# Choosing the branch hint in the middle of a product: a TensorE program that jumps between eleven copies of an expert's code

## What is computed

```
gate = jnp.minimum(xb @ w_gate[e] + b_gate[e], SWIGLU_LIMIT)
up = jnp.clip(xb @ w_up[e] + b_up[e], -SWIGLU_LIMIT, SWIGLU_LIMIT)
act = gate * jax.nn.sigmoid(SWIGLU_ALPHA * gate) * (up + 1.0)
y = act @ w_down[e] + b_down[e]
```

## Time and profile before

| what | value |
|---|---|
| median of 3 runs | 2039.57 us (2031.48, 2039.57, 2040.16) |
| the profiled execution, its own time | 2035.33 us |
| its span from first to last instruction | 2033.6 us |
| granted clock of TensorE, mean | 0.987 |
| PE busy | 1957.0 us, 96% of the span |
| the expert stage | from about 506 to 2017 us |

### The profile page before, as it was taken

How to read it: one execution, slowest core, us unless ns; L and a number is a source line. 1 busy time by engine, 2 the same in 40 slices (tenths; PEclk the granted TensorE clock), 3 DMA queues, 4 the chain that set the end, 5 groups by cost and what they waited for, 6 DMA issues and landing times.

```text
span 2033.6 us, 40238 instructions
## 1 busy us (share of the span) xinstructions
PE 1957.0 (96%) x17569; PEld 1578.1 (78%) x17570; DVE 571.7 (28%) x1108; ACT 283.8 (14%) x457; POOL 283.1 (14%) x481
## 2 busy tenths in 40 slices
PE   8999988998899999999999999999999999999996
PEld 4444456555897798889778999987987878889996
DVE  3115667354222121222212222222221222121214
ACT  2001245111001001101100111111010110100103
POOL 0001233176101000000000010010000000101003
PEclk9999999998999999999999999999999999999998
DMA  4210021312978889998999988899999998887855
GB/s 176 84 42 1 1 94 44 127 69 95 330 264 301 307 277 339 336 326 290 356 348 336 314 300 283 294 359 350 313 351 322 335 347 292 282 280 250 288 170 202
DMA packets 232704, 501.98 MB, mean 247 GB/s; under 512 B 8822, under 2 KB 9487, under 8 KB 232498
## 3 DMA queue, kind: packets, MB, share of 16 engines
q1 hardware_dynamic: 219024, 454.53, 62.3%
q0 software_dynamic: 13424, 44.36, 8.9%
q10 hardware_dynamic: 50, 0.01, 0.0%
HBM read 463.70 MB, written 35.23 MB: 245 GB/s over the span
## 4 chain that ended last, share of the span: by engine, by line
PE 92%; issue 3%; DVE 2%; DMA 2%; ACT 1%; SPq 0%; POOL 0%; POOLq 0%; DVEq 0%
PE ps L1742 33%; PE ps L1751 23%; PE ps L1778 12%; PE ps L1515 8%; PE ps L1653 5%; PE ps L1509 3%; PE ps L1765 2%; PE ps L1553 1%; PE ps L1771 1%; DVE soft L1056 1%; ACT hT L782 1%; DMA qk<-x_rows 1%; PE ps L1673 1%; PE ps L1592 0%; DMA w_ring<-in_w_in 0%
## 5 line engine op out<-in xcount | busy, mean ns | idle before, releaser
L1751 PEld LDWEIGHTS ps<-hT,qk 128*64 128x64 f32 x4608 | 234.0, 138 | 26.9 <-issue 26.4
L1751 PE MATMUL ps<-hT,qk 128*64 128x128 f32 (+3 forms) x4608 | 239.1, 266 | 15.6 <-issue 13.8
L1778 PE MATMUL ps<-w_ring,hT 128*128 128x512 f32 x576 | 251.8, 593 | 0.0
L1742 PE MATMUL ps<-hT,qk 128*128 128x136 f32 (+5 forms) x1792 | 236.1, 295 | 9.4 <-issue 9.4
L1742 PEld LDWEIGHTS ps<-hT,qk 128*128 128x128 f32 x1792 | 234.4, 193 | 13.0 <-issue 13.0
L1742 PE MATMUL ps<-hT,w_ring 128*128 128x136 f32 (+5 forms) x1792 | 235.4, 292 | 2.9 <-DVE x L1303 1.5
L1742 PEld LDWEIGHTS ps<-hT,w_ring 128*128 128x128 f32 x1792 | 230.9, 190 | 5.2 <-issue 4.6
L1778 PEld LDWEIGHTS ps<-w_ring,hT 128*128 128x128 f32 x576 | 107.5, 190 | 126.7 <-issue 126.3
L609 POOL DMA_INDIRECT x_rows<-x,hT x44 | 70.3, 1598 | 788.2 <-ACT x L887 385.6
L1515 PE MATMUL ps<-hT,w_ring 128*128 128x512 f32 x384 | 168.9, 595 | 1.3 <-DMA w_ring<-in_w_in 1.3
L1281 DVE TENSOR_TENSOR hT<-ps,early 128x512 f32<-128x512 f32 (+1 forms) x64 | 51.7, 808 | 414.6 <-PE ps L1742 208.3
(11 more groups left out here) (261 smaller groups left out, 1667.3 us busy)
## 6 DMA issues: line engine op xcount, KB each, us to landing
w_ring<-in_w_down SPq DMA_DIRECT2D x64, 2048.0 KB, 8.9
qk<-in_w_gate SPq DMA_DIRECT2D x32, 2048.0 KB, 8.3
qk<-in_w_up SPq DMA_DIRECT2D x32, 2048.0 KB, 10.5
v<-in_w_gate SPq DMA_DIRECT2D x32, 2048.0 KB, 10.6
u_all<-in_w_up SPq DMA_DIRECT2D x32, 2048.0 KB, 9.6
x<-in_b_down SPq DMA_DIRECT2D x32, 512.0 KB
w_ring<-in_w_in SPq DMA_DIRECT2D x3, 2048.0 KB, 8.9
x<-in_x SPq DMA_DIRECT2D x8, 512.0 KB, 9.5
```

Of the source, the lines that this page charges most:

```text
L1742: ins = pe.matmul(bank[:, m, 0:n], w[g][:, k, m * P:(m + 1) * P], rhs[:, k, 0:n], start=k == 0, stop=k == KC - 1)
L1751: ins = pe.matmul(bank[part, m, 0:n], w[g][:, k, m * P + part.start:m * P + part.stop], rhs[:, k, 0:n], start=k == 0, stop=k == KC - 1)
L1778: ins = pe.matmul(ps[:, 2 * (g % PAIRS), :], aT[:, k, 0:P], w[g][:, k, :], start=k == 0, stop=k == KC - 1)
```

## The change

The decision tree moves. It now stands between the two parts of product 4, ahead of the wait at line 1873, runs over all twelve targets (the eleven widths and the end) in every case, and isn't split by `ONE_BLOCK` any more. Behind product 4 stays only the second turn, where the next expert is wide.

```
                         product(4, aT, early)
                     else:
                         rows_of(4, range(KC // 2))
+
+                    hints = {}
+                    call(hints, after, 0, len(WIDTHS))
                     pe.wait_ge(a_ready, e * 2 + 2)
                     pe.sem_inc(passed, 1)
                     (product(4, aT, late) if two_blocks else rows_of(4, range(KC // 2, KC))).then_inc(group_done, 1)
 
-                    hints = {}
                     with pe.If(after > ONE_BLOCK):
-                        with pe.If(after > len(WIDTHS) - 1):
-                            call(hints, after, len(WIDTHS), len(WIDTHS))
-                        with pe.Else():
+                        with pe.If(after < len(WIDTHS)):
                             pe.wait_ge(xT_ready, 2 * e + 3)
                             pe.sem_inc(passed, 1)
                             turn_in(1).then_inc(turn_mm[1], 1)
-                            call(hints, after, ONE_BLOCK + 1, len(WIDTHS) - 1)
-                            pe.sem_inc(passed, 1)
                         pe.sem_inc(passed, 1)
                     with pe.Else():
                         pe.sem_inc(turn_mm[1], 1)
-                        call(hints, after, 0, ONE_BLOCK)
                     ready(5)
```

## The result

The changed kernel takes 2016.19 us (median of 5 runs, 2014.49 to 2018.40) against 2036.12 (5 runs, 2031.48 to 2040.16) of the kernel before on the same chips: a ratio of 0.990, interval 0.9889 to 0.9911. Its profiled execution has a span of 2012.8 us, 20.8 under the span before.

The account below looks back on a forecast made before the run. PE is busy 1957.0 of 2033.6 us; code-fetch gaps at body heads and their half-clock stretches cost 24 us. Terms -2.3 - 2.6 - 1.7 - 4.1 + 7.0 + 1.0 + 1.5 + 0.9 = -0.3; forecast 2036, range 2022 to 2046.

Parts of the forecast that it names:

- Step 1: Between the second turn and product 5: the tree leaves, PE's gaps at seven wide-to-wide exits go, -2.3 us.
- Step 2: The tree's new place in product 4: PE's queued work covers its 1.4 us, cost 0.
- Step 3: Wide tails, boundary earlier through six added instructions a body: 168->96 -2.6, 144->120 -1.7, 168->144 -4.1 us.
- Step 4: 108 body's branch chain past a boundary, hint and branch apart: +7.0 us at one 108->128, +1.0 at 108->96.
- Step 5: Entries of the 128 and 160 bodies: shorter first blocks give less cover, +1.5 and +0.9 us.
- Step 6: Two 96->128 exits: branch's block entered 1.3 us earlier, worth 5.3 us each or nothing; taken as 0.
- rival A: At body exits, the hint acts when issued, wherever its branch stands; nearly all head gaps go: 2011 to 2015, chance 0.12.
- B: As forecast, but the two 96->128 exits gain from an earlier fetch: -11 us, 2024 to 2026, chance 0.12.
- if the 96->128 gaps vanish: Sign in the profile after, at the heads of the 128 body: gaps gone there would mean the hint-acts-earlier rivals hold.
- Step 7: Last exit, 180->end: early fetch lost, but the end waits on output DMAs; cost 0, at worst 2.6 us.
- C: Slower: double misses at narrow exits and 160 entries, wide-tail gains absent: +25 us, 2060, chance 0.08.
- D: Only two blocks are held, so hinted blocks are pushed out at up to 13 wide exits: +49 us, 2084, chance 0.02.

Follow-up runs that it names:

- l6_late: Kernel before with six more counter increments in product 4 of every body, so bodies start as in the changed kernel, hint where it was: ratio 0.9906.
- part 3: Changed kernel with the 128 body moved back by 2, 4 and 6 instructions by the code's length: 2014.07, 2012.78 and 2013.12 us.
- m128_s20: Changed kernel with never-run code placed to move only the 128 body 20 instructions back in its block, by the code's length: 2028.67 us.
- m128_s8: Changed kernel with never-run code placed to move only the 128 body 8 instructions back in its block, by the code's length: 2029.93 us.
- al128: Changed kernel with never-run code making every body whole blocks long, each starting in the middle of a block: 2044.11 us.
- al8_head: `al8` with 100 of its unused instructions moved ahead of the first tree, so the first body's hint and branch share a block: 2004.26 us.
- l0_early: Changed kernel with six increments fewer in each body's tree, so bodies start as in the kernel before, hint early: ratio 0.9967.
- al8: Changed kernel with never-run code making every body whole blocks long, each starting on a block boundary by the stalls' count: 2008.42 us.

## Why the prediction was wrong

**Held.** Step 1: the tree's seven gaps ahead of product 5 are gone. The runs give the whole move of the tree as 1.1 (within the noise), 4.1 and 6.1 us in three layouts, where I had 2.3. Step 2, cost 0: nothing in the timeline speaks against it. Step 3 held: the gaps at 168->96 (two), 144->120 (of which it had left 0.5) and 168->144 went, and the half-clock stretch behind the last of them too. They went in `l6_late` as well, where only the layout was changed.

**Step 4 failed**, the +7.0 and +1.0 at the 108 exits. No gap came at the first 108->128; its last branch took 0.47 us:

```profile
L1806 PEldq COMPARE_BRANCH  x4: 67/72/465, 793.1 to 793.5; - x4
```

I had fixed all positions by one stall in the 128 body, and carried it over to bodies ahead of it. But by the rule of part 3, in the kernel before the 120 body would begin 5 ahead of a boundary and is moved, so that the 96 and 108 bodies stand 5 instructions lower than my count had them. With that the taken branch of the changed 108 body stands 2 instructions ahead of the boundary and not behind it, in the block of its hint.

**Step 5 failed**, +1.5 and +0.9. I had the 128 body 4 instructions and the 160 body 8 ahead of a boundary; each would begin within 16 of one (10 and 4 by the corrected count) and is moved onto it. In place of the shortest first block the 128 body got the longest. This one error is worth most of the 20 us: 12.5 and 13.7 by `m128_s20` and `m128_s8`, against a sum that had it as a loss.

**Step 6**, 0 for the two 96->128 exits, was right about the branch, which still lasts 6.3 us, and wrong about the gap. The 7.2 us of cover hide a miss of 6.3; what they don't hide is the second miss behind a short first block. The gap of 4.55 was the second block all along, as I had written in step 4, and it was in step 5 that it could have gone. My sign for rival A or B, "if the 96->128 gaps vanish", was therefore no sign of either.

**Step 7**, 0 and at worst 2.6, measures 1.7 (2.30 us against 0.55 behind the last body). What no step had: the first body's second block, 0.64 before and 3.72 after, since the 136 body stands 29 instructions further on, 24 by code and 5 by the moves ahead of it; and 1.6 us more inside the 96 body.

**Rival A** came near the time, 2011 to 2015 for 2016.2, and missed the cause. The hint moved by 2 to 7 us, as the forecast has it, and brought little of the 20, and `al128` and `al8_head` show that an early hint isn't acted on while its branch is in a later block. That part of the forecast's reading stands, and it is now shown by a matched pair instead of by a sorting of exits. **B** had the 96->128 gaps go by an earlier fetch, and the branch there is as late as before. **C** had the kernel slower. **D** fell with the earlier trace rows already. Also, the next block is asked for when a block is entered, not at its end. In the kernel after, the 128 body begins at 662 us, on a boundary, and the 126 matmuls of its first block keep PE until about 669.9 (240 of them take 13.32 us); the instruction queue brings the next block between 665.3 and 665.8:

```profile
q8 instruction: 1, 0.02, 14.1%
```

The Trainium skill (Runtime: NRT & Kernel Launch, Instruction fetch mechanics) says that the sequencer fetches the next page while it executes the current one, and the trace agrees. That is why a block of 7 us of work hides a fetch of 6.3, and a first block of 18 or 30 instructions hides next to nothing of it.

What stays open: who moves the bodies. The Trainium skill says in the same section that the runtime puts markers into the stream at block boundaries, which would be a place where such a move is made, but no run here shows one. Open too is why the gap at 160->128 went with the earlier hint alone in `l0_early`, and whether the hint's 1.1 us in the new layout are anything but noise.

## What to carry over

In a program that jumps between bodies of code longer than a block, place each body so that it begins on a block boundary, and its hint in the block of its branch; measure a change of a few instructions against a copy that is filled up to the same length, or the layout will be read as the effect. A position that was calibrated by one stall holds only around that stall: count the instructions up to several stalls, in several bodies, before placing a boundary within ten instructions. And where a branch waits long and PE doesn't, look at what the cover was spent on next.

## What the runs showed of the hardware

- By the counts of stalls and fetches a body that would begin up to 16 instructions ahead of a boundary of 256 begins on the boundary; from 17 on it doesn't (16, 14, 12, 11, 10 and 5 moved; 17, 18, 30 and 35 not).
- The layout alone moved this kernel by 36 us, 1.8%, between `al8` and `al128`.
- A hint with its branch in the same block was followed by its fetch in 1.4 us where the DMA engines were nearly idle (`al8_head`, busy share 0.04 from 498 to 500 us), and in 4.1 at 108->128 in the kernel before, where they were full; with its branch in a later block it waited 12.4 us (`al8`).
- No hints at the ends of the bodies cost 37 us against the changed kernel (`l6_none`, 2053.61 us).
- A branch to code that isn't held, with no hint acted on in time, lasts 6.3 us among the weight transfers; PE idled for 4.55 us behind it before the change and not at all after, by the length of the target's first block alone.
